# A hybrid trunk kernel: context and latent scores placed beside the expert rows, and gated units of two tiles in one slot, twice

## What is computed

```python
def mixer_odd(h, w_pw1, b_pw1, w_dw, b_dw, ln_g, ln_b, w_pw2, b_pw2):
    u = h @ w_pw1 + b_pw1
    u = u[..., :D_CONV] * jax.nn.sigmoid(u[..., D_CONV:])     # gated units
    u = depthwise_conv(u, w_dw) + b_dw                        # 31 taps
    u = jax.nn.silu(layernorm(u, ln_g, ln_b, LN_EPS))
    return u @ w_pw2 + b_pw2

def one(xb):                       # peer: one block of 128 tokens
    q = (xb @ w_q).reshape(BLOCK, PEER_HEADS, D_QUERY)
    s1 = jnp.einsum('thd,hnd->thn', q[..., :half], keys[0])
    s2 = jnp.einsum('thd,hnd->thn', q[..., half:], keys[1])
    ...                            # top 16 of each, top 16 of their sums: eidx, sv
    g = jax.nn.softmax(sv, axis=-1)
    act = jax.nn.gelu(jnp.einsum('thkd,td->thk', u_tab[eidx], xb), approximate=False)
    wgt = g * act
    return jnp.einsum('thk,thkd->td', wgt, v_tab[eidx])
```

## Time and profile before

| | |
|---|---|
| median of 3 runs | 4683.55 us (4677.9 to 4689.87) |
| the profiled execution, its own time | 4694.33 us |
| its span in the profile | 4692.5 us |
| busy: PE / DVE / ACT / POOL | 3236.1 / 2775.4 / 1728.1 / 1468.9 us |
| mean granted PE clock | 0.853 |
| moved by DMA, read from HBM | 1567.70 MB, 1559.88 MB |
| of these by the gathers of POOL | 1342.45 MB |
| loads `wq` (queries), `wq` (second matrix), `wg` | 112, 40, 80 times 512 KB |

### The profile page before, as it was taken

One profiled execution on the slowest core, in us unless ns is written; L12 is line 12 of the kernel. 1 busy time (PEld: TensorE's weight loads), 2 busy tenths in 40 slices (PEclk: granted clock), 3 DMA queues, 4 the chain that ended last, 5 costly groups with the idle time before them and its releaser, 6 DMA issues. The chain is left out here.

```text
span 4692.5 us, 72376 instructions
## 1 busy us (share of the span) xinstructions
PE 3236.1 (69%) x27071; PEld 1615.7 (34%) x27071; DVE 2775.4 (59%) x7104; ACT 1728.1 (37%) x5320; POOL 1468.9 (31%) x1298
## 2 busy tenths in 40 slices
PE   7988787777755556666665775786677677666555
PEld 4533676443211113323332332452344244223111
DVE  1257544335556766765656776585576776665764
ACT  1036222023222324544323553463454354332332
POOL 0000000012334443443334343343344443433443
PEclk9996898888877778988888887897898898888777
DMA  5161001268899999999999999999999999999998
GB/s 215 52 259 47 18 4 48 90 220 331 335 363 406 421 420 413 419 413 375 385 419 416 419 418 385 379 419 419 378 385 420 417 419 417 413 419 418 412 420 334
DMA packets 241982, 1567.70 MB, mean 334 GB/s; under 512 B 29942, under 2 KB 31057, under 8 KB 71265
## 3 DMA queue, kind: packets, MB, share of 16 engines
q0 software_dynamic: 184768, 1342.45, 69.8%
q1 hardware_dynamic: 56424, 220.51, 12.2%
q10 hardware_dynamic: 442, 0.12, 0.0%
HBM read 1559.88 MB, written 3.10 MB: 333 GB/s over the span
## 5 line engine op out<-in xcount | busy, mean ns | idle before, releaser
L1554 POOL DMA_INDIRECT t_ring<-in_peer_uv,t_eidx x1280 | 1461.4, 1142 | 3181.7 <-PE t_ps L2164 2051.3
L2160 PE MATMUL t_ps<-t_ring,t_dg 64*64 64x512 f32 x2560 | 1584.0, 751 | 1145.4 <-ACT t_dg L1840 1107.5
L1680 DVE SCALAR_TENSOR_TENSOR t_ring<-t_ring,t_hring 128x1024 f32<-128x1024 f32 x1024 | 1253.6, 1224 | 841.5 <-DMA t_ring<-in_peer_uv,t_eidx 810.3
L2164 PE MATMUL t_ps<-t_ring,t_dg 64*64 64x512 f32 x2560 | 1601.7, 758 | 0.0
L2163 PE MATMUL t_ps<-t_ring,t_dg 64*64 64x512 f32 x2560 | 1601.4, 758 | 0.0
L2161 PE MATMUL t_ps<-t_ring,t_dg 64*64 64x512 f32 x2560 | 1601.0, 758 | 0.0
L2160 PEld LDWEIGHTS t_ps<-t_ring,t_dg 64*64 64x64 f32 x2560 | 347.9, 157 | 2093.3 <-issue 2063.7
L1829 ACT ACTIVATE t_wgt<-t_dots 128x2 f32<-128x2 f32 x640 | 130.2, 203 | 1872.9 <-DVE t_ring L1680 1824.4
L1680 DVE SCALAR_TENSOR_TENSOR t_ring<-t_ring,t_early 128x1024 f32<-128x1024 f32 x256 | 313.8, 1226 | 313.8 <-DMA t_ring<-in_peer_uv,t_eidx 312.3
L1840 ACT ACTIVATE t_dg<-t_eye,t_wgt 128x64 f32<-128x64 f32 x1280 | 376.8, 340 | 2.7 <-ACT t_wgt L1834 1.9
L2164 PEld LDWEIGHTS t_ps<-t_ring,t_dg 64*64 64x64 f32 x2560 | 349.0, 157 | 0.0
(11 more groups left out here) (367 smaller groups left out, 4465.3 us busy)
## 6 DMA issues: line engine op xcount, KB each, us to landing
t_wq<-in_peer_w_q SPq DMA_DIRECT2D x112, 512.0 KB
ev_mod_ring<-in_mod_w SPq DMA_DIRECT2D x48, 1024.0 KB, 10.0
t_wg<-in_cv_w_pw SPq DMA_DIRECT2D x80, 512.0 KB
t_ring<-in_peer_uv,t_eidx POOLq DMA_INDIRECT x1280
t_wq<-in_cv_w_pw SPq DMA_DIRECT2D x40, 512.0 KB
t_pair<-modrows SPq DMA_DIRECT2D x25, 512.0 KB
ev_wring<-in_ab_w_in SPq DMA_DIRECT2D x21, 512.0 KB, 3.6
ev_qk<-in_ab_w_out SPq DMA_DIRECT2D x1, 4096.0 KB, 12.1
```

What stands on the lines that cost most here:

```text
L1554: pool.indirect_dma_start(ring[:, place[n], :], None, table, bass.IndirectOffsetOnAxis(ap=eidx[:, s % 2, r:r + 1], axis=0)).then_inc(row_i ...
L1680: V.scalar_tensor_tensor(ring[:, place[n], 0:D], ring[:, place[n], 0:D], 1.0, h_of(j), ALU.mult, ALU.mult, accum_out=dots[:, j % 2, r:r + ...
L2160: nc.tensor.matmul(straight[low, cols], dg[low, n % DIAGS, :], ring[low, one, rows], **ends)
L2164: second = nc.tensor.matmul(crossed[low, cols], dg[high, (n + 1) % DIAGS, :], ring[high, two, rows], **ends)
```

## The change

It does three things.

1. The context blocks become a side of their own: blocks 0 to 3 stay ahead of the transposes (tick -2), blocks 4 to 7 follow them (tick -1), then comes the first exponential, and blocks 8 to 16 (the last only copies and scores) go into slot 0 at ticks 0, 3, up to 24.
2. The latent blocks begin at tick 26 and end at 114, 5.5 ticks apart. Each block's eight products are issued as two halves two ticks apart, and ACT's copies four ticks after the first half.
3. The tiles form groups (0, 1), (2, 3) and (4), in slots 2, 4 and 6. The two norms of a group are at bases 4 and 12; its two transposed tiles lie side by side (`both`), and a product has 256 columns. A block of units comes every 6 ticks from tick 22 on (4 for the single tile), with one sigmoid for both tiles and one product for each. The convolutions of slots 2 and 4 begin at tick 72. Convolution and post keep their slots. Buffers move within `early`, which now holds `hT1` too.

```diff
     JOBS = 2 * NT
     LEAD, NPE, BATCH = 2, 5, 8
     TAPS = NPE * CONVW
-    GLU_SLOT = lambda i: i + 2
+    GROUPS = ((0, 1), (2, 3), (4,))
+    group = lambda i: i // 2
+    GLU_SLOT = lambda i: 2 + 2 * group(i)
     CONV_SLOT = lambda i: (2, 4, 5, 6, 7)[i]
...
-    score_tick = lambda b: max(0, 6 * (b - 2))
+    ctx_tick = lambda b: -2 if b < 4 else -1 if b < 8 else 3 * (b - 8)
+    score_tick = lambda b: 26 + 2 * (11 * b // 4)
...
+    glu_tick = lambda g, b: 22 + (6 if len(GROUPS[g]) == 2 else 4) * b
+    conv_tick = lambda i: 72 if CONV_SLOT(i) in (2, 4) else 58
+    glu_base = lambda i: 4 if i in (0, 2) else 12
...
+    units_in = lambda i: KD * (1 + (group(min(i + 1, NT - 1)) if i else 0))
...
-        early = sb("early", [P, 8672])
...
-        cv = early[:, 5600:6624].rearrange("p (k c) -> p k c", k=KD)
+        cv = early[:, 7648:8672].rearrange("p (k c) -> p k c", k=KD)
+        both = early[:, 7648:9696].rearrange("p (t k c) -> p k t c", t=2, k=KD)
...
-        diag = early[:, 7648:7648 + BATCH * P].rearrange("p (n c) -> p n c", c=P)
-        hT1 = sb("hT1", [P, KD, P])
+        diag = early[:, 5600:5600 + BATCH * P].rearrange("p (n c) -> p n c", c=P)
+        hT1 = early[:, 8672:9696].rearrange("p (k c) -> p k c", k=KD)
...
-                if GLU_SLOT(i) == s:
+                if GLU_SLOT(i) == s and i != 3:
                     PAIRS["norm", i] = len(PAIRS)
...
-                def for_glu(i):
-                    yield 2
-                    load_pair(("norm", i), mod_row(i, 1), mod_row(i, 0))
+                def for_glu(g):
+                    for i in GROUPS[g]:
+                        yield glu_base(i) - 4
+                        if i != 3:
+                            load_pair(("norm", i), mod_row(i, 1), mod_row(i, 0))
                     for b in range(KD):
-                        yield 18 + 4 * b
+                        yield glu_tick(g, b) - 6
                         for a in range(2):
-                            n = 2 * (KD * i + b) + a
+                            n = 2 * (KD * g + b) + a
                             if n >= 2:
                                 sp.wait_ge(S["wg_used"], n - 1)
                             sp.dma_start(wg[:, a].rearrange("p k c -> p (k c)"), io["cv_w_pw1"][0, a * KD + b]).then_inc(wg_in[a], 16)
...
                 def norm_one(i):
-                    yield 14
+                    yield glu_base(i) + 2
                     mean(NORMS["norm", i])
-                    yield 16
+                    yield glu_base(i) + 4
                     invert(NORMS["norm", i])
                     dve.wait_ge(S["pair_in"], 32 * (PAIRS["norm", i] + 1))
+                    if i:
+                        dve.wait_ge(S["turned1"], i)
                     m = own(V.scalar_tensor_tensor(y, x[:, i, :], rstd[:, NORMS["norm", i]:NORMS["norm", i] + 1], pair[:, 0, :], ALU.mult, ALU.mult))
-                    yield 18
+                    yield glu_base(i) + 6
                     after_own(m)
                     V.tensor_tensor(y, y, pair[:, 1, :], ALU.add).then_inc(S["h1_done"], 1)
                     dve.wait_ge(S["h1_done"], i + 1)
-                    dve.sem_inc(S["pair_used"], 1)
-
-                def gated_units(i):
-                    col = glu_col(i) + PADC
+                    if i != 2:
+                        dve.sem_inc(S["pair_used"], 1)
+
+                def gated_units(g):
                     for b in range(KD):
-                        yield 24 + 4 * b + 6
-                        n = KD * i + b
+                        yield glu_tick(g, b) + 6
+                        n = KD * g + b
                         dve.wait_ge(S["sig_done"], n + 1)
                         bias = VEC["cv_b_pw1"] + b
-                        V.scalar_tensor_tensor(glu[:, b, col:col + P], banks[:, 4 + b % 2, 0:P], K.vec[:, bias:bias + 1], sg[:, b % 2, :],
-                                               ALU.add, ALU.mult).then_inc(S["glu_done"], 1)
+                        for e, i in enumerate(GROUPS[g]):
+                            col = glu_col(i) + PADC
+                            last = V.scalar_tensor_tensor(glu[:, b, col:col + P], banks[:, 4 + b % 2, e * P:(e + 1) * P], K.vec[:, bias:bias + 1], sg[:, e, :],
+                                                          ALU.add, ALU.mult)
+                        last.then_inc(S["glu_done"], 1)
...
-                    yield 61
+                    yield conv_tick(i) + 3
...
-                    yield 12
+                    yield glu_base(i)
                     act.wait_ge(S["summed"], GLU_SLOT(i))
-                    act.wait_ge(S["var_done"], done_by(POST_SLOT, GLU_SLOT(i)))
-                    square(y, i, NORMS["norm", i])
-                    yield 15
+                    act.wait_ge(S["q_done"], Q0 + NC * done_by(POST_SLOT, GLU_SLOT(i) - 1))
+                    dst = turned_tile(i)
+                    square(dst, i, NORMS["norm", i])
+                    yield glu_base(i) + 3
                     root(NORMS["norm", i])
-                    yield 21
+                    yield glu_base(i) + 9
                     act.wait_ge(S["turned1"], i + 1)
-                    act.wait_ge(S["q_done"], Q0 + NC * done_by(POST_SLOT, GLU_SLOT(i) - 1))
-                    nc.scalar.copy(hT1[:].rearrange("p k t -> p (k t)"), ps[:, 2, :]).then_inc(S["hTa_done"], 1)
-
-                def sigmoids(i):
+                    nc.scalar.copy(dst, ps[:, 2, :]).then_inc(S["hTa_done"], 1)
...
+                def sigmoids(g):
                     for b in range(KD):
-                        yield 24 + 4 * b + 3
-                        n = KD * i + b
+                        yield glu_tick(g, b) + 4
+                        n, members = KD * g + b, len(GROUPS[g])
                         act.wait_ge(S["g_done"], n + 1)
-                        if n >= 2:
-                            act.wait_ge(S["glu_done"], n - 1)
+                        if n:
+                            act.wait_ge(S["glu_done"], n)
                         bias = VEC["cv_b_pw1"] + KD + b
-                        nc.scalar.activation(sg[:, b % 2, :], banks[:, 4 + b % 2, P:2 * P], ACT.Sigmoid, bias=K.vec[:, bias:bias + 1]).then_inc(S["sig_done"], 1)
+                        nc.scalar.activation(sg[:, 0:members, :], banks[:, 4 + b % 2, 2 * P:(2 + members) * P].rearrange("p (t c) -> p t c", c=P),
+                                             ACT.Sigmoid, bias=K.vec[:, bias:bias + 1]).then_inc(S["sig_done"], 1)
...
+                    act.wait_ge(S["g_done"], KD * last_group(POST_SLOT(i)))
+                    nc.scalar.copy(early[:, 8672:9696], ps[:, 3, :]).then_inc(S["hTb_done"], 1)
...
-                        yield score_tick(b)
+                        yield score_tick(b) + 4
...
+                def context_scores():
+                    for b in range(NC + 1):
+                        yield ctx_tick(b) + (2 if b >= 8 else 0)
+                        if b < NC:
+                            act.wait_ge(S["q_done"], b + 1)
+                            nc.scalar.copy(qT1[:, b % 2, :], banks[:, 6 + b % 2, 0:P]).then_inc(S["q_copied"], 1)
+                        if b:
+                            act.wait_ge(S["s_done"], b)
+                            nc.scalar.copy(s01[:, 0, (b - 1) // 2, (b - 1) % 2, :], banks[:, 4 + (b - 1) % 2, 0:P]).then_inc(S["s_copied"], 1)
+
                 turned(0, 2)
-                for b in range(NC + 1):
-                    if b < NC:
-                        act.wait_ge(S["q_done"], b + 1)
-                        nc.scalar.copy(qT1[:, b % 2, :], banks[:, 6 + b % 2, 0:P]).then_inc(S["q_copied"], 1)
-                    if b:
-                        act.wait_ge(S["s_done"], b)
-                        nc.scalar.copy(s01[:, 0, (b - 1) // 2, (b - 1) % 2, :], banks[:, 4 + (b - 1) % 2, 0:P]).then_inc(S["s_copied"], 1)
+                context = Side(context_scores())
+                context.run(-2)
                 turned(2, 2 * NT)
+                context.run(-1)
                 Side(exponents(0)).run(0)
...
+                        sides += [context, Side(latent_scores())]
...
-                def queries(n, rhs, out):
+                def queries(n, rhs, out, first=0, end=KD):
                     pe.wait_ge(wq_in[n % 2], 16 * (n // 2 + 1))
-                    for k in range(KD):
+                    for k in range(first, end):
                         last = nc.tensor.matmul(out, wq[:, n % 2, k, :], rhs[:, k, :], start=(k == 0), stop=(k == KD - 1))
+                    if end < KD:
+                        return
                     last.then_inc(S["wq_used"], 1)
                     pe.wait_ge(S["wq_used"], n + 1)
                     pe.sem_inc(S["q_done"], 1)
...
                         yield score_tick(b)
                         if b < NC:
+                            if b == 0:
+                                pe.wait_ge(S["s_copied"], NC)
                             if b >= 2:
```

(28 more changed lines are left out.)

38 lines of the change are left out of this document (21 added, 17 removed).

## The result

The kernel after takes 4501.07 us (median of 4 runs, 4497.7 to 4509.8) where the kernel before takes 4680.73 (4 runs, 4677.7 to 4689.9): a ratio of 0.9616, 95% interval 0.9596 to 0.9636. It is 180 us faster. The profiled execution took 4501.9 us with a span of 4500.1, so the spans differ by 192.4 us. That is about 13 more than the medians differ by, since the profiled execution of before (4694.3) lay 14 over its median.

What follows compares the result with a forecast made beforehand. DMA bytes bound most slots, with bubbles in slots 3, 5 and 6 and a slow slot 0; -55 + 3.6 - 38.9 + 1.1 - 38.4 - 3 = -130.6 us gave 4553 us, range 4508 to 4620.

Steps and rivals of the forecast that it cites:

- Part 2: Loop of slot 0 with its new context steps and latent blocks: -2 us for ticks 6 to 26, 0 for 26 to 118.
- Ticks 26 to 118: Slot 0's picks beside split latent blocks: 2.80 us a pick plus 2.4 a block, 296 us, change 0 (-18 to +26).
- First pair: Start of slot 0: earlier first exponential brings the first pair of picks on PE to 949.5 from 1002.3, -53 us.
- Ticks 6 to 26: Slot 0's picks beside eight context steps: 3.2 us a pick, 64 us, change -2 (-6 to +4).
- Gated units in pairs: Three groups instead of five: 16.8 MB less wg; slots 3 and 5 -38.9 and -38.4, 2 and 4 +3.6 and +1.1.
- Doubled units at nothing: Slots 2 and 4: doubled units cost 0, since 12.8 us of PE a block is covered by 17.6 us of DMA.
- the slower rival: PE at its lower clock in slots 2 and 4 loses up to 214 us; time 4767 at most; chance 0.04.
- More comes back than I count: Rival: split blocks cost only their load (-18), head start 58, slot 6 -16; 4514 us; chance 0.13.
- Slot 0 gives its head start back: Rival: half blocks cost as whole ones (+26), context loads come late; slot gains 18 or less, 4590 us; chance 0.17.
- doubled units stall: Rival: the doubled units stall slots 2 and 4, +19 us each, 4591 us; chance 0.13.
- doesn't do what it says: Rival: exponential stays late, slots 2 and 4 lose what 3 and 5 win; within 14 us of before; chance 0.03.
- the variance wait: Slot 6: its norm no longer waits for the variance product, where ACT stood 5.79 us; -3 us (-6 to 0).

Runs made afterwards that it cites:

- run 6: Kernel before with only the latent blocks' queries split in halves and ACT's copy four ticks later, at their old ticks: 4637.4 us.
- run 3: Kernel after with each latent block's eight products in one piece again, ACT's copy still four ticks later: 4538.2 us.
- run 4: Kernel after with each latent block's products in one piece and ACT's copy in the same tick, at the new ticks: 4556.2 us.
- run 5: Kernel after with the halves kept, but ACT's copy at the tick of the second half: 4520.0 us.
- Run 11: Kernel before with seven more 0.52 MB loads, which nothing reads, between picks 80 and 122 of slot 0: 4676.0 us.
- run 10: Kernel after without an edit, timed again beside the kernel before: 4507.7 us, ratio to before 0.9624.
- Run 9: Kernel after with context blocks 0 to 4 ahead of the first exponential, blocks 5 to 16 in slot 0 every two ticks: 4510.7 us, ratio to before 0.9635.
- kernel 2: Kernel after without its slot 0 edits, so grouped gated units alone: 4597.9 us, ratio to before 0.9819.
- run 1: Kernel before with only the slot 0 edits (context, first exponential, latent blocks in halves with late copy): 4593.4 us, ratio 0.9812.
- run 8: Kernel after with ACT's wait for the variance product put back in slot 6: 4517.1 us.
- run 7: Kernel after with the four products of each latent block's first half done twice on PE: 4537.9 us.

## Why the prediction was right or wrong

**The step that failed is the second item of Part 2, "Ticks 26 to 118".** It put the price of a split block at 2.4 us, "at least the load, 0.524 MB / 418 GB/s = 1.25 us", so 0 in sum, -18 at the least. It was -35.6 in the first profiles, and -23 to -36 between any of three kernels with the old blocks at their old ticks and five with the new. Two things were wrong in it.
- *The price of a split block.* It is 0.4 to 0.7 us (run 6 and the kernels with sixteen such blocks), not 2.4. I had put the new price near the middle between the load and the 4.0 us of a whole block, as if part of those 4.0 were work that two halves keep. Nearly none of it was. It was the hold and the copy: run 3 shows what the long piece costs (+25 to +30), runs 4 and 5 what the early copy costs (+16 with whole blocks, +17 to +23 with halves), all at the same work. The reading behind it, argued from the code: six rows at 2.8 us a pick leave 17 us from a gather's issue to the end of its pair, and 7.13 us of PE in one piece (8.3 with the scores behind it), or ACT standing 12 us at a copy, is more than what gather, dot, weights and pair leave over of that, while 3.6 us (4.8 with the scores behind the second half) is not. The slack itself wasn't measured.
- *The floor.* The load's 1.25 us were added to a pace at which DMA had idle time (0.95 in the earlier trace rows). Run 11 shows that loads in such a stretch cost nothing that can be seen. The floor by bytes alone was 92 x 1.0486 + 16 x 0.524 = 104.9 MB at 418 GB/s = 251 us, 45 under before. The pace without blocks is a second floor, 92 x 2.76 = 254. The stretch took 260.1, at 403 GB/s. My lowest bound for it, 278, was thus 24 us over the higher of the two, and the low end of the whole range was too high with it.

**First pair**: right. -51 for -53; the exponential came at 940.2 for 943 to 945 and the pair at 944.6 for 949.5, but the first gather, too, was 6.8 us earlier, which no edit did; of the two late loads that I counted one came, 6.16 us. In run 10 the first gather is at 928.3, as before, and the exponential and the pair come at 944.8 and 949.2. Run 9 shows that little more is to be had here: the dots of the first rows are next.

**Ticks 6 to 26**: -6.3 for -2, at the good end of its bounds (-6 to +4). Part of it is spread: kernels 2 and 11 have the old code there and take 62.1 and 61.8 us, not 65.8. 20 picks take 2.98 us each for the 3.2 that I took, so context blocks of 3.1 us at every third tick cost little too.

**Gated units in pairs**: right in what it does and in the sum, -86.7 for -75.6 over slots 2 to 6. These slots take 1802.0 to 1810.0 us in nine profiles with the grouped units and 1884.1 to 1890.8 in four without, so -74 to -89. Slots 3 and 5 fell by 35.3 and 30.8, not 38.9 and 38.4; they are not quite their twins 8 and 7, as loads for the slots behind them go out ahead. By bytes (rate times length) slot 5 moved 152.3 MB where slot 7 moved 149.9 in the earlier trace rows, so 5.8 of the 7.6 us between them are bytes. Slots 4 and 6 went from 347.0 to 341.1 and from 399.5 to 384.9, where I had +1.1 and -3. Neither is safe: kernel 11, with the old slot 4, has 340.4, and run 10, with the new slot 6, has 392.5. Slots 5 and 6 together fell by 39 to 49 us, where I had 41.4. Over slots 2 to 6 the bytes fell by 16.0 MB (16.8 worked out), 38 us; the other 48 were bubbles. The slots taken one by one were thus less right than their sum. Slot 2 was 349.0, not 352.7; the 3.6 us that I had added for its second norm and pair of rows don't show, and no run says why.

**Doubled units at nothing**: right. The Trainium skill ("TensorE: Matmul & The Clock Gate", HAM oscillation) describes a PE that waits for DMA between bursts and falls back to its low clock, which was the slower rival. Here slots 2 and 4 show 0.89 and 0.93 and last 349.0 and 341.1 us. Their units (by form, in the windows of slots 2 and 4 of the kernel after; busy us, mean ns, idle time ahead) took 3.9 and 3.75 us a half of sixteen matmuls, where I had 3.7, and waited for no load:

```profile
L2099 PE MATMUL t_ps<-t_early,t_wg 128*128 128x256 f32 x256 | 62.4, 399 | 0.0
L2099 PE MATMUL t_ps<-t_early,t_wg 128*128 128x256 f32 x256 | 60.0, 388 | 0.0
```

So the waits for DMA that the page describes did not arise at the units, and these slots don't test its rule.

**The rivals.** "More comes back than I count" (0.13, 4514) named what happened in slot 0, split blocks at less than I took. Its -16 for slot 6 isn't settled (-4 to -15 in nine profiles). The time came out lower still, since its split blocks had the same floor. "Slot 0 gives its head start back", "doubled units stall", the low clock and "doesn't do what it says" did not come true: 26 to 118 took 260, not over 320, slots 2 and 4 stay under 360, and runs 1 and 2 show both halves at work.

**The clock.** It is 1.00 in picks 26 to 118 where it was 0.84. Run 6 has 0.89 there and takes 257.9 us, less than the kernel after. Run 5 has 0.96 and takes 282.7, run 10 has 0.97 and takes 263.1. So it mostly goes along with the gain and doesn't make it. For the whole blocks at new ticks (0.93 and 0.91) no run holds it fixed, and up to 13.6 of the 25 to 30 us of kernel 3 could be its.

**Open**: the worth of the variance wait (run 8); how the loss of run 7 divides between a long hold and a full PE; the slack of the ring, which no run measured; and the size of small differences in picks 26 to 118, since three kernels with the old blocks show 288.3, 292.2 and 295.7 us there, and five with the new 260.1 to 265.3. The differences argued from above are all larger than that, but for the few tenths in the price of a block and for whether the early copy costs more with halves than with whole blocks. The 6.8 us ahead of the first gather are spread of executions, as the other profiles show, and not a gain. Slot 6 keeps its two waits of 16.7 and 8.8 us; a version without them wasn't tried. None of these kernels beats the kernel after.

## What to carry to other kernels

Where in-order engines feed a short ring, look at how long a block put in front of a step holds it in one piece, and not only at its work: the same work in two pieces instead of one was worth 25 to 30 us here. Cut it in pieces (3.6 and 4.8 us here) and let the engine that reads the result come to it after it is done, not with it. Where the trace shows a transfer engine idle beside a steady pace, added bytes are free until its share is full, so the floor of such a stretch is all its bytes at full rate, and not the old pace plus the new bytes. A forecast for stages that load ahead for each other should be made over their sum.

## What the runs showed of the hardware that I had not expected

- One core's DMA moved 417 GB/s over the 349 us of slot 2 and up to 421 in slices of 112 us, nearly all of it read from HBM. The Trainium skill ("DMA: Bandwidth & Descriptors", Where 436 GB/s comes from) has some 358 as the bound for such transfers; no run here shows that bound. The Trainium skill's page "HBM Reference" (Specifications (TRN2)) agrees with the runs: it has some 425 for a core that streams alone.
- Six loads of 0.52 MB between 34 gathers brought 362 GB/s to 401 and cost no time that could be measured (92.2 for 93.8 us).
- The granted clock of PE was 1.00 over the 260 us of picks 26 to 118 in the kernel after, with waits between its bursts (224 us busy), and 0.97 in the same code in run 10. With the same work in whole blocks it was 0.93 (290 us) and 0.91 (307 us). It did not follow the time: run 6 took 258 us at 0.89.
- The same code up to the first gather, a fifth of the span, reached its end anywhere from 920.5 to 928.3 us.
